# Second expert matrices of a mixture-of-experts stage loaded in 2 MB pieces with 16 KB runs, activations transposed with a stride of four features

## What is computed

```python
logits = h @ w_router + b_router
top_val, top_idx = lax.top_k(logits, 4)
gates = softmax(top_val)
# for each expert e, with its tokens xb (rows of h):
u = xb @ w1[e] + b1[e]                  # w1[e]: 1024 x 2048
glu = minimum(u[:, 0::2], 7.0)
lin = clip(u[:, 1::2], -7.0, 7.0)
act = glu * sigmoid(1.702 * glu) * (lin + 1.0)
y = act @ w2[e] + b2[e]                 # w2[e]: 1024 x 1024
out[token] += gate * y
```

## Time and profile before

| | us |
|---|---|
| median of 3 runs | 2309.51 |
| lowest, highest | 2307.12, 2314.98 |
| the profiled execution, its own time | 2312.77 |
| its span in the trace | 2311.0 |
| mean granted clock of TensorE | 0.979 of full |

### The profile page before, as it was taken

How to read it: one execution, slowest core, us unless ns; L and a number is a source line. 1 busy time by engine, 2 the same in 40 slices (tenths; PEclk the granted TensorE clock), 3 DMA queues, 4 the chain that set the end, 5 groups by cost and what they waited for, 6 DMA issues and landing times.

```text
span 2311.0 us, 34017 instructions
## 1 busy us (share of the span) xinstructions
PE 2213.1 (96%) x15007; PEld 1368.3 (59%) x15008; DVE 706.0 (31%) x1186; ACT 357.4 (15%) x771; POOL 100.3 (4%) x114
## 2 busy tenths in 40 slices
PE   7999999999999998989998998999999999999997
PEld 6767686888577775567887653344344444434432
DVE  0000101621275415347777532112111121121113
ACT  1000200240100012243434111001000010100000
POOL 1000000000100000112221000000000000000000
PEclk9999899999999999999999989999999999999999
DMA  9655444244678951000001379999999999999996
GB/s 319 192 158 184 145 138 145 82 137 161 221 237 273 285 189 55 1 3 3 3 22 48 149 313 419 426 426 424 417 424 426 425 426 411 417 425 426 425 425 271
DMA packets 199428, 582.13 MB, mean 252 GB/s; under 512 B 9620, under 2 KB 153808, under 8 KB 166384
## 3 DMA queue, kind: packets, MB, share of 16 engines
q1 hardware_dynamic: 194656, 564.70, 63.5%
q0 software_dynamic: 4208, 13.27, 1.5%
q10 hardware_dynamic: 416, 1.96, 0.2%
HBM read 576.49 MB, written 3.42 MB: 251 GB/s over the span
## 4 chain that ended last, share of the span: by engine, by line
PE 90%; DVE 5%; DMA 2%; ACT 1%; issue 1%; SPq 0%; ACTq 0%; DVEq 0%
PE ps L2561 22%; PE ps L605 13%; PE ps L2573 10%; PE ps L664 8%; PE ps L614 7%; PE ps L1333 5%; PE ps L2540 3%; PE ps L2588 2%; PE ps L795 2%; PE ps L768 2%; PE ps L1660 2%; PE ps L1680 1%; PE ps L1762 1%; PE ps L969 1%; DMA arena<-in_w 1%; PE ps L1677 1%
## 5 line engine op out<-in xcount | busy, mean ns | idle before, releaser
L2561 PE MATMUL ps<-ring,const 128*64 128x512 f32 (+1 forms) x1536 | 472.0, 594 | 0.8 <-ACT const L2315 0.8
L2561 PEld LDWEIGHTS ps<-ring,const 128*64 128x64 f32 (+1 forms) x1536 | 160.6, 144 | 307.4 <-issue 306.1
L605 PE MATMUL ps<-arena,ring 128*128 128x256 f32 x1408 | 313.4, 381 | 2.6 <-issue 2.6
L605 PEld LDWEIGHTS ps<-arena,ring 128*128 128x128 f32 x1408 | 264.7, 190 | 47.3 <-issue 12.9
L2561 PE MATMUL ps<-arena,const 128*64 128x512 f32 (+1 forms) x512 | 225.2, 593 | 0.0
L2573 PE MATMUL ps<-ring,const 128*64 128x512 f32 (+1 forms) x768 | 190.3, 594 | 0.8 <-DMA ring<-in_w 0.8
L664 PE MATMUL ps<-arena,ring 128*128 128x256 f32 x800 | 174.5, 381 | 1.3 <-issue 1.3
L664 PEld LDWEIGHTS ps<-arena,ring 128*128 128x128 f32 x800 | 153.0, 191 | 22.5 <-issue 1.5
L2775 DVE TENSOR_SCALAR arena<-ps 128x1024 f32<-128x1024 f32 x18 | 22.0, 1225 | 458.5 <-PE ps L2561 458.4
L614 PE MATMUL ps<-ring,arena 128*128 128x512 f32 x352 | 157.6, 592 | 0.0
L2573 PEld LDWEIGHTS ps<-ring,const 128*64 128x64 f32 (+1 forms) x768 | 65.2, 143 | 112.6 <-issue 111.1
(11 more groups left out here) (485 smaller groups left out, 2458.8 us busy)
## 6 DMA issues: line engine op xcount, KB each, us to landing
ring<-in_w SPq DMA_DIRECT2D x96, 2048.0 KB, 17.7
ring<-in_w SPq DMA_DIRECT2D x96, 1024.0 KB, 15.2
arena<-in_w SPq DMA_DIRECT2D x32, 2048.0 KB, 19.9
ring<-in_w_in SPq DMA_DIRECT2D x26, 1536.0 KB, 6.9
arena<-in_w SPq DMA_DIRECT2D x32, 1024.0 KB, 17.5
ring<-in_w_ada SPq DMA_DIRECT2D x16, 1536.0 KB, 9.0
ring<-in_ffn_w_gate SPq DMA_DIRECT2D x44, 512.0 KB, 4.0
ring<-in_ffn_w_up SPq DMA_DIRECT2D x44, 512.0 KB, 5.4
```

The lines of the kernel that those rows point to most:

```text
L605: ins = pe.matmul(ps[:, j % 2, half * S:(half + 1) * S], s[:, col0:col0 + P], uT[:, k, :], start=(k == 0), stop=(k == KD - 1))
L2561: ins = pe.matmul(ps[a * n:(a + 1) * n, q, :], xsT[:, k, a * n:(a + 1) * n], chunk(chunks[a])[:, q * 512:(q + 1) * 512], start=False, stop ...
```

## The change

Three things change together. A second matrix is loaded in two pieces of 2 MB instead of four of 1 MB: a piece takes two neighbouring chunks, holds four features to a partition (4p to 4p+3 of 512), and a partition reads 16 KB in one run. The new function `w2_chunk` says which chunk holds step c of expert a, in the same way as `w1_chunk` does for the first matrices; the tables of uses and landings follow. SyncE waits for room for both chunks of a piece before it issues it, and TensorE waits for landings before the steps c = 0 and 2 only, there for the pieces of all experts of the group. And since a partition holds four neighbouring features, the activations are transposed with a stride of four columns instead of two. The first matrices, the gather, and everything outside the expert stage stay as they are. `more`, for experts with more tokens than they have rows, is changed alike.

```diff
+def w2_chunk(s, c, a):
+    w = len(BLOCKS[s])
+    return W2_AT[s] + 2 * (c // 2 * w + a) + c % 2
...
         def w2_load(e, n, expert, c):
-            e.dma_start(chunk(n).rearrange("p (j n) -> p j n", j=2),
-                        x["w2_2"][0, expert, 2 * c * P:2 * (c + 1) * P, :].rearrange("a (p j) n -> p (a j) n", j=2)).then_inc(*landing(n))
+            e.dma_start(chunk(n, 2).rearrange("p (j n) -> p j n", j=4),
+                        x["w2_2"][0, expert, 4 * c * P:4 * (c + 1) * P, :].rearrange("a (p j) n -> p (a j) n", j=4)).then_inc(*landing(n))
...
-                    for c in range(KD // 2):
+                    for c in range(KD // 4):
                         for a, r in enumerate(blk):
-                            n = W2_AT[s - 1] + c * len(blk) + a
-                            room(n)
+                            n = W2_AT[s - 1] + 2 * (c * len(blk) + a)
+                            room(n + 1)
                             w2_load(e, n, expert[r], c)
...
-                ins = pe.transpose(banks(6, 2)[:, j * P:(j + 1) * P], act_[:, j // 2 * 2 * P + j % 2:(j // 2 + 1) * 2 * P:2], ident)
+                ins = pe.transpose(banks(6, 2)[:, j * P:(j + 1) * P], act_[:, j // 4 * 4 * P + j % 4:(j // 4 + 1) * 4 * P:4], ident)
...
                 for c in range(KD // 2):
-                    for a in range(w):
-                        moe_landed(pe, W2_AT[s] + c * w + a)
-                    for ins in down_pe(pe, w, c, W2_AT[s] + c * w):
+                    chunks = [w2_chunk(s, c, a) for a in range(w)]
+                    for n in chunks:
+                        if c % 2 == 0:
+                            moe_landed(pe, n)
+                    for ins in down_pe(pe, w, c, chunks):
                         ins.then_inc(*up("m_used"))
```

More of the change, by code:

```diff
@@ L112, in chunk_tables @@
         if s:
-            for i in range(KD // 2 * len(BLOCKS[s - 1])):
-                used[W2_AT[s - 1] + i] = len(used) + 1
+            for c in range(KD // 2):
+                for a in range(len(BLOCKS[s - 1])):
+                    used[w2_chunk(s - 1, c, a)] = len(used) + 1
     for s in range(NBLK + 1):
         pieces = [W1_AT[s] + i for i in range(0, KD * len(BLOCKS[s]), 2)] if s < NBLK else []
-        pieces += [W2_AT[s - 1] + i for i in range(KD // 2 * len(BLOCKS[s - 1]))] if s else []
+        pieces += [W2_AT[s - 1] + i for i in range(0, KD // 2 * len(BLOCKS[s - 1]), 2)] if s else []
         for n in pieces:
@@ L2525, in more @@
                     w1_load(e, 2 * c, one, c)
-                for c in range(KD // 2):
-                    w2_load(e, KD + c, one, c)
+                for c in range(KD // 4):
+                    w2_load(e, KD + 2 * c, one, c)
             moe_more(e, turns, most_tokens(e), more)
@@ L2564, in up_pe, with down_pe @@
                         yield ins
-        def down_pe(pe, w, c, at_):
+        def down_pe(pe, w, c, chunks):
             for j in range(2):
@@ L2572, in down_pe @@
                         lo = j * D + nh * 512
-                        ins = pe.matmul(ps[a * n:(a + 1) * n, 4 + nh, :], actT[:, 2 * c + j, a * n:(a + 1) * n], chunk(at_ + a)[:, lo:lo + 512],
+                        ins = pe.matmul(ps[a * n:(a + 1) * n, 4 + nh, :], actT[:, 2 * c + j, a * n:(a + 1) * n], chunk(chunks[a])[:, lo:lo + 512],
                                         start=(c == 0 and j == 0), stop=(c == KD // 2 - 1 and j == 1))
@@ L2698, in more @@
                 for c in range(KD // 2):
-                    more_landed(pe, KD + c, n)
-                    for ins in down_pe(pe, 1, c, KD + c):
+                    if c % 2 == 0:
+                        more_landed(pe, KD + c, n)
+                    for ins in down_pe(pe, 1, c, [KD + c]):
                         if c == KD // 2 - 1:
```

## The result

The changed kernel takes 2313.53 us in the median of 20 runs against 2307.82 for the kernel before, also 20 runs; the ratio is 1.0018 with a 95% interval of 1.0011 to 1.0025, some 4.2 us (the two medians are 5.7 us apart). It is slower, by less than the 0.3% that were called no change, and it is the first rival of the prediction (2315 us), not its forecast (2323). The forecast's main term, 14 us for the stride of four, isn't there.

A forecast was written before the change was run, and what follows sets the result against it. TensorE was taken to bound the expert stage, with the DMA queue equally full. Stride 14.0, minus 3.2 of waits, plus 2.5 of coarse wait gave +13.3 us over the 2309.5 median, 2323 us; range 2311 to 2328.

The forecast's parts named there:

- first rival: Transposes in the expert stage: stride of four free or nearly, total +5.4 us, 2315 us; chance 0.33.
- What bounds the kernel: Expert stage: TensorE and DMA both full, TensorE only just behind the queue; load changes give back at most 3.2 us.
- Part 1: Second-matrix loads: 16 KB runs raise the queue from 422 to 426 GB/s, −3.0 us of queue time.
- Part 2: SyncE's wait for room for both chunks delays pieces where the queue is short: +5 us (0 to 14).
- four places: Three queue dips (379 to 410 GB/s) and the first second matrix, where late issue costs 1.2 us each.
- Part 3: Second product, last two groups: TensorE's coarser data waits; with the loads' and room's effects, +5.4 us (+1 to +10).
- Part 4: Eight activation transposes per group, 144 in all: stride of four costs 0.097 us a load, +14.0 us (bounds 0, 17.0).
- The sum: Expert stage: 14.0 for the stride, −3.2 for vanished waits, +2.5 for the last stages' coarse wait: +13.3 us.
- old waits: TensorE's three waits for weights in the kernel before, 3.2 us in all, said to vanish if TensorE gets slower.

The follow-up runs named there:

- wait_and_room: Changed kernel with second matrices in 1 MB pieces of 8 KB runs, both coarse waits (room and data) kept; ratio 1.0023 to the kernel before.
- coarse_room: Changed kernel with 1 MB halves in 2 MB-piece order, each issued when both chunks are free, data awaited each step; ratio 1.0009 to the kernel before.
- stride_alone: Changed kernel's layout and stride of four, but second matrices in 1 MB pieces, room and landing awaited for each; ratio 1.0000 to the kernel before.
- coarse_wait: Changed kernel with 1 MB pieces, room awaited for each, but TensorE awaiting two steps' data before steps 0 and 2; ratio 1.0015 to the kernel before.
- stride_8: Changed kernel with its transposes reading at a step of eight columns instead of four; ratio 1.0012 to the kernel before.
- coarse_wait4: Changed kernel with 1 MB pieces, room awaited for each, but TensorE awaiting all four steps' data before step 0; ratio 1.0096 to the kernel before.

## Why the prediction was wrong

**What bounds the kernel** held. TensorE is the bound in all stages but the ends of the pairs, and by the expert time no kernel here gained more than the 3.2 us that it had waited (the best is 2.7 below).

**Part 1** (longer runs, −3.0 us) was right in kind: 428 against 422 GB/s, which is 4.4 us of queue by the windows where 3.0 were said, and 2.2 us at the last landing (wait_and_room against the changed kernel).

**Part 2** (the room) was right that the four places get worse, but sized too high: +5 us on the queue. At the last landing the room with the order of issue cost 1.5 us (coarse_room) to 2.0 (wait_and_room), and the new places in the store perhaps 0.7. With the runs' −2.2 the last landing moved by +0.4 us in all; the +2 us net that I carried into part 3 should have been that. And the deepest of the four, 360 GB/s, isn't the coarse room's doing, as stride_alone has it too.

**Part 3** (the wait for data) held. 17th group: waits of 4.9 and 2.9 us said, 2.70 and 2.69 measured. The first is 2.2 us smaller, half because the data came earlier than said (0.9 us later than before, not 2) and half because TensorE came to them 1.0 us later (2257.34 − 2.70 − 1397.97 against 2257.99 − 1402.35). 18th: 1.2 said, 0.83 measured, with 7.1 us behind it. What it left out is the clock, which can fall to half in such a wait: it did in coarse_wait, and not in the changed kernel's trace. Parts 1 to 3 said +5.4 us; the expert time is 3.9 longer and the ratio says 4.2.

**Part 4** is the step that failed: without it parts 1 to 3 alone gave +5.4. The term of 144 x 0.097 = +14.0 us measured next to nothing (a load 2 to 3 ns longer, eight transposes 0.01 us; stride_alone 0.7 us in all with its other places in the store). I had bounds of 0 and 17.0 us and took the nearest row with a long step as the value. That row was VectorE's reduction L2400, of another engine, with a group ending every four elements, which I named as a doubt and then didn't weigh. The row of TensorE itself, eight transposes at 1.04 us and eight at 1.22, said that a doubling of the step costs at most 22 ns a load. The argument that TensorE takes its elements faster than VectorE and so must suffer more was an argument without a row. What the runs show in its place: 1.09, 1.22, 1.23, 1.16 us for steps of 1, 2, 4 and 8. Nor does it hold that a longer step can't gain: eight is cheaper than two.

Of the Trainium skill's two sentences the trace now decides. Loads of 211 ns at a step of four against 208 at two show no price for single hits; the rule of two hits on a line (Advanced Engine Details and Errata, SBUF Cachelines) doesn't agree with this for TensorE's weight loads in float32, and the one rise that there is, from 140 to 208 ns, lies between steps of one and two, which both have two hits on a line. The note of SBUF — State Buffer, also of the Trainium skill, that four fp32 are a free stride agrees, but by stride_8, 193 ns, neither does the price begin beyond four.

**The sum** said that with a slower TensorE the old waits vanish; that was never put to the test, as TensorE wasn't slower. **The rivals:** the first one, the stride being free, came in with its mechanism and near its size (+5.4 us said; +3.9 by the traces, +4.2 by the ratio), and I had given it 0.33 against 0.52. That size is in part luck, as the room (+5 us against 1.5 to 2.0) and the gain of the runs (−3.0 against −2.2) were both set too high and cancel in part. The measured 2313.5 us lies at the low side of the range only because the range reached down for that rival; the forecast of +13.3 us was three times the change, and the chance of 0.60 for slower by over 0.3% stood on it. (By its own terms, 0.52 + 0.05 + 0.06, that chance was 0.63.)

## What to carry to other kernels

Where two resources are both full, a change that helps one of them by 1% is paid at the few places where the other catches it: look for the end of the stretch in which the queue falls back, and count the work that stands behind the last landing. When a test of one part costs more than the part can explain, look at the clock behind its waits, and compare last landings before ends. A load can be large, but what is awaited at once should be small there; two groups of eighteen held four fifths of this loss, and the order of heavy and light groups alone was worth 2.7 us, two thirds of it. When an unknown price has a row on its own engine and a row on another, take the own engine's, even if its step is smaller.

## What the runs showed of the hardware

The weight load of a float32 transpose takes 140 ns at a unit step, 208 to 211 at steps of two and four and 193 at a step of eight. That eight is cheaper than four I have no reason for. In or just behind waits of 2.7 to 9.5 us for data TensorE's granted clock fell to half in some cases (coarse_wait, coarse_room, stride_8, coarse_wait4) and not in others (2.70 and 2.69 us in the changed kernel); 32 matmuls then took up to 10.06 us in place of 7.1. At 128 partitions and 1 to 2 MB a load, the queue moves 428, 422 and 408 GB/s in runs of 16, 8 and 4 KB.
